# Raw and scaled evictions, token mixing by pairs of tiles, and a new order of steps beside a projection

## The reference

```python
p = p + (token_shift(p) - p) * mu            # token_shift: the row of the token before, 0 for the first
r, k, v, wd, ad, gd = _split(p, (512, 512, 512, 64, 64, 128))
w_log = -softplus(-(w0 + tanh(wd) @ w_up)) - 0.5
decay = exp(-exp(w_log))
a = sigmoid(a0 + ad @ a_up)
g = sigmoid(gd) @ g_up
kk = hd(k * k_k)
kk = kk * rsqrt(maximum(sum(kk * kk, axis=-1), 1e-24))    # keys of unit length, by head of 64
k_mod = hd(k * (1.0 + (a - 1.0) * k_a))
y = rwkv7_scan(r, decay, k_mod, v, -kk, kk * a)           # a recurrence over the tokens
bonus = sum(r * k_mod * r_k, axis=-1) * v
```

## Time and profile before

| | us |
|---|---|
| median of 3 runs | 3233.77 (3233.0 to 3235.81) |
| the profiled execution, its own time | 3229.9 |
| its span in the trace | 3228.1 |
| mean granted clock of TensorE | 0.915 of full |
| TensorE busy | 2859.5 (89% of the span) |
| DVE busy | 1922.0 (60%) |
| ACT busy | 1361.9 (42%) |

### The profile page before, as it was taken

How to read it: one execution, slowest core, us unless ns; L and a number is a source line. 1 busy time by engine, 2 the same in 40 slices (tenths; PEclk the granted TensorE clock), 3 DMA queues, 4 the chain that set the end, 5 groups by cost and what they waited for, 6 DMA issues and landing times. The chain is left out here.

```text
span 3228.1 us, 53616 instructions
## 1 busy us (share of the span) xinstructions
PE 2859.5 (89%) x23052; PEld 2452.1 (76%) x23052; DVE 1922.0 (60%) x2576; ACT 1361.9 (42%) x1873; POOL 151.7 (5%) x116
## 2 busy tenths in 40 slices
PE   7898678999897778999998998889999989988899
PEld 6787557888786657888886875678888878756688
DVE  5754766965655766956555444666565644446564
ACT  5413334645413244645453232545454532325443
POOL 0030000000030000000000310000000012000000
PEclk9998888998898888998998998989999988989899
DMA  5211114564111123555542111245645411203453
GB/s 213 92 40 53 66 54 148 197 212 157 66 43 63 66 81 137 202 187 183 198 144 74 40 66 40 93 143 202 220 170 197 141 64 40 72 34 119 138 201 131
DMA packets 54667, 386.18 MB, mean 120 GB/s; under 512 B 6688, under 2 KB 7328, under 8 KB 8352
## 3 DMA queue, kind: packets, MB, share of 16 engines
q1 hardware_dynamic: 54432, 382.76, 34.5%
HBM read 381.69 MB, written 1.05 MB: 119 GB/s over the span
## 5 line engine op out<-in xcount | busy, mean ns | idle before, releaser
L320 PE MATMUL banks<-normed_high,weights_high 128*128 128x256 f16 (+1 forms) x4096 | 1150.7, 281 | 49.6 <-DVE normed_low L414 22.6
L321 PE MATMUL banks<-normed_low,weights_high 128*128 128x256 f16 (+1 forms) x4096 | 1149.7, 281 | 0.0
L322 PE MATMUL banks<-normed_high,weights_low 128*128 128x256 f16 (+1 forms) x4096 | 1148.1, 280 | 0.0
L306 DVE SCALAR_TENSOR_TENSOR weights_low<-weight_ring,weights_high 128x2048 f16<-128x2048 f32 x334 | 761.1, 2279 | 417.2 <-ACT weights_high L300 402.8
L300 ACT ACTIVATE weights_high<-weight_ring 128x2048 f16<-128x2048 f32 x306 | 580.2, 1898 | 299.3 <-PE banks L322 284.0
L320 PE MATMUL banks<-projected,weights_high 128*128 128x256 f16 x1696 | 471.7, 278 | 73.3 <-DVE projected L331 73.3
L320 PEld LDWEIGHTS banks<-normed_high,weights_high 128*128 128x128 f16 (+1 forms) x4096 | 412.8, 101 | 126.3 <-issue 47.3
L321 PE MATMUL banks<-projected,weights_high 128*128 128x256 f16 x1696 | 471.8, 278 | 0.0
L322 PE MATMUL banks<-projected,weights_low 128*128 128x256 f16 x1696 | 471.3, 278 | 0.0
L322 PEld LDWEIGHTS banks<-normed_high,weights_low 128*128 128x128 f16 (+1 forms) x4096 | 411.9, 101 | 59.6
L321 PEld LDWEIGHTS banks<-normed_low,weights_high 128*128 128x128 f16 (+1 forms) x4096 | 411.3, 100 | 59.2 <-issue 1.8
(11 more groups left out here) (390 smaller groups left out, 3251.8 us busy)
## 6 DMA issues: line engine op xcount, KB each, us to landing
weight_ring<-w SPq DMA_DIRECT2D x356, 1024.0 KB, 4.9
small_weights<-small SPq DMA_DIRECT2D x2, 1280.0 KB, 7.9
constants<-const SPq DMA_DIRECT2D x1, 1601.0 KB, 10.1
weight_ring<-w SPq DMA_DIRECT2D x2, 640.0 KB, 3.8
residual<-xt SPq DMA_DIRECT2D x1, 1024.0 KB, 5.0
small_weights<-small SPq DMA_DIRECT2D x2, 512.0 KB, 10.4
out<-residual SPq DMA_DIRECT2D x4, 256.0 KB, 2.8
parameters<-par SPq DMA_DIRECT2D x2, 115.5 KB, 9.6
```

The source lines that it names most:

```text
L306: nc.vector.scalar_tensor_tensor(out=self.part(self.mem.w_low, g), in0=self.part(self.mem.ring, g), scalar=W_SCALE, in1=self.part(self.mem ...
L320: pe.matmul(out, w_high, high, start=start, stop=False, skip_group_check=skip)
L321: pe.matmul(out, w_high, low, start=False, stop=False, skip_group_check=skip)
L322: return pe.matmul(out, w_low, high, start=False, stop=stop, skip_group_check=skip)
```

## The change

1. For tiles 0 to 13 ACT evicts twice: a raw tile (into `raw`, tiles 18 to 31 of the scratch memory) and a tile scaled by `(1 - mu)` times the constant of the halves, one value for each partition (`keep`, made once by DVE in `mu_kept`).
2. The mixing is `projected[t] += mu * raw[t-1]`, one DVE instruction for a tile and 255 tokens, two tiles after each of the low halves 3 to 9. The difference of all 14 tiles (L1205) and the negation of the first token (L1206) are gone.
3. `keys_squared` goes from 11 to 7 on DVE, `keys_sum` from 10 to 6 on TensorE, `keys_guarded` from 14 to 9, `keys_root` from 13 to 7 on ACT (ahead of `low_rank_in`), `keys_inverse` from 15 to 10, `keys_spread` from 14 to 11. `gates_of_a` goes from 9 to 8 and `exps` from 12 to 11 on ACT; `decays_summed` and `decays_centred` from 12 and 13 to 11 and 12; `keys_mixed` and `bonus_products` to 13, `keys_unit` to 14, `bonus_values` to 15, `operands_near` to 16 on DVE; `bonus_sum` from 15 to 13 on TensorE.
4. Two copies of `operands_far` (L1296) go from DVE to ACT, behind the high halves at the end (`operands_copied`).

```diff
@@ project_stage, DVE
         loaded(dve)
+        for step in beside.vector.get("begin", ()):
+            step(link, say, need)
...
@@ project_stage, ACT
             act.wait_ge(sig("tiles_done"), i + 1)
+            if i == 0 and beside.keep is not None:
+                need("mu_kept", 1)
             for n, (g, c0, m, part, tile) in enumerate(grp):
-                ins = nc.scalar.activation(mem.proj[part:part + m, tile, :],
-                                           mem.ps[part:part + m, i % BANKS, n * T:(n + 1) * T],
-                                           ACT.Copy, scale=PART_X)
+                got, scale = mem.ps[part:part + m, i % BANKS, n * T:(n + 1) * T], PART_X
+                if beside.keep is not None and tile < 14:
+                    nc.scalar.activation(beside.raw[:, tile, :], got, ACT.Copy, scale=PART_X)
+                    scale = beside.keep[:, tile:tile + 1]
+                ins = nc.scalar.activation(mem.proj[part:part + m, tile, :], got, ACT.Copy,
+                                           scale=scale)
...
@@ Rwkv
-        self.vector = {9: [self.shift_low_rank], 10: [self.shift], 11: [self.keys_squared],
-                       12: [self.decays_summed], 13: [self.decays_centred],
-                       14: [self.keys_guarded, self.keys_mixed],
-                       15: [self.keys_inverse, self.bonus_products], 16: [self.keys_unit],
-                       "end": [self.bonus_values, self.operands_near, self.operands_far,
-                               self.operands_state]}
-        self.scalar = {7: [self.low_rank_in], 9: [self.gates_of_a], 12: [self.exps],
-                       13: [self.keys_root], "end": []}
-        self.tensor = {8: [self.low_rank_up], 10: [self.keys_sum], 14: [self.keys_spread],
-                       15: [self.bonus_sum], "end": []}
+        self.keep = cut(14)
+        self.raw = cut.buffer[:, 18 * T:32 * T].rearrange("p (a t) -> p a t", a=14)
+        self.vector = {"begin": [self.mu_kept],
+                       3: [self.shift(0)], 4: [self.shift(2)], 5: [self.shift(4)],
+                       6: [self.shift(6)], 7: [self.shift(8), self.keys_squared],
+                       8: [self.shift(10)], 9: [self.keys_guarded, self.shift(12)],
+                       10: [self.keys_inverse], 11: [self.decays_summed],
+                       12: [self.decays_centred], 13: [self.keys_mixed, self.bonus_products],
+                       14: [self.keys_unit], 15: [self.bonus_values], 16: [self.operands_near],
+                       "end": [self.operands_far, self.operands_state]}
+        self.scalar = {7: [self.keys_root, self.low_rank_in], 8: [self.gates_of_a],
+                       11: [self.exps], "end": [self.operands_copied]}
+        self.tensor = {6: [self.keys_sum], 8: [self.low_rank_up], 11: [self.keys_spread],
+                       13: [self.bonus_sum], "end": []}
...
+    def mu_kept(self, link, say, need):
+        mu = self.mem.par[:, C1["mu"]:C1["mu"] + 14]
+        say(self.nc.vector.tensor_scalar(self.keep, mu, -PART_X, PART_X, ALU.mult, ALU.add), "mu_kept")
+
+    def shift(self, first):
+        def step(link, say, need):
+            need("bank_free", first // 2 + 1)
+            for i in (first, first + 1):
+                p = self.mem.proj[:, i, 1:T]
+                say(self.nc.vector.scalar_tensor_tensor(out=p, in0=self.raw[:, i, 0:T - 1],
+                                                        scalar=self.col("mu", i), in1=p,
+                                                        op0=ALU.mult, op1=ALU.add), "shifted")
+        return step
...
+    def operands_copied(self, link, say, need):
+        for i, (n4, f4) in enumerate(self.halves()):
+            need("near_ready", i + 1)
+            link(self.nc.scalar.copy(f4[:, :, 1, :], n4[:, :, 1, :]))
...
     def low_rank_in(self, link, say, need):
-        need("shifted", 2)
+        need("shifted", 14)
...
     def keys_sum(self, pe, need):
-        need("decay_sigmoid", 4)
         need("kk_squares", 1)
...
     def keys_spread(self, pe, need):
+        need("decay_sigmoid", 4)
         need("kk_inverse", 1)
```

More of the change, by code:

```diff
@@ L1171, in __init__ @@
         self.bonus, self.gate, self.out = mem.y[:, 4:8, :], mem.y[:, 8:12, :], mem.y[:, 0:4, :]
-        self.mixed = cut.buffer[:, 0:14 * T].rearrange("p (a t) -> p a t", a=14)
-        self.vector = {9: [self.shift_low_rank], 10: [self.shift], 11: [self.keys_squared],
-                       12: [self.decays_summed], 13: [self.decays_centred],
-                       14: [self.keys_guarded, self.keys_mixed],
-                       15: [self.keys_inverse, self.bonus_products], 16: [self.keys_unit],
-                       "end": [self.bonus_values, self.operands_near, self.operands_far,
-                               self.operands_state]}
-        self.scalar = {7: [self.low_rank_in], 9: [self.gates_of_a], 12: [self.exps],
-                       13: [self.keys_root], "end": []}
-        self.tensor = {8: [self.low_rank_up], 10: [self.keys_sum], 14: [self.keys_spread],
-                       15: [self.bonus_sum], "end": []}
+        self.keep = cut(14)
[12 more added lines that the diff above has]
+                       13: [self.bonus_sum], "end": []}
     def two(self, b):
@@ L1197, in q64 @@
         return flat(ap).rearrange("p (q t) -> p q t", t=HD)
[L1201 to L1207, removed]
-    def shift(self, link, say, need, tiles=tuple(range(12))):
-        for i in tiles:
-            p = self.mem.proj[:, i, :]
-            say(self.nc.vector.scalar_tensor_tensor(out=p, in0=self.mixed[:, i, :],
-                                                    scalar=self.col("mu", i), in1=p,
-                                                    op0=ALU.mult, op1=ALU.add), "shifted")
+    def mu_kept(self, link, say, need):
[10 more added lines that the diff above has]
+        return step
     def keys_squared(self, link, say, need):
@@ L1288, in operands_near, with halves @@
                              q64(self.p_r), q64(z[7]), ALU.mult))
-        link(V.tensor_tensor(flat(self.bt), flat(z[1]), flat(z[5]), ALU.mult))
-        link(V.tensor_tensor(flat(self.kt), flat(self.p_k), flat(z[5]), ALU.mult))
+        say(V.tensor_tensor(flat(self.bt), flat(z[1]), flat(z[5]), ALU.mult), "near_ready")
+        say(V.tensor_tensor(flat(self.kt), flat(self.p_k), flat(z[5]), ALU.mult), "near_ready")
+    def halves(self):
+        return [[v.rearrange("p a (b q t) -> p (a b) q t", b=2, q=2) for v in pair]
+                for pair in ((self.bt, self.btp), (self.kt, self.ktp))]
+    def operands_copied(self, link, say, need):
+        for i, (n4, f4) in enumerate(self.halves()):
+            need("near_ready", i + 1)
+            link(self.nc.scalar.copy(f4[:, :, 1, :], n4[:, :, 1, :]))
     def operands_far(self, link, say, need):
         V = self.nc.vector
-        for near, far in ((self.bt, self.btp), (self.kt, self.ktp)):
-            n4, f4 = (v.rearrange("p a (b q t) -> p (a b) q t", b=2, q=2) for v in (near, far))
-            link(V.tensor_copy(f4[:, :, 1, :], n4[:, :, 1, :]))
+        for n4, f4 in self.halves():
             link(V.tensor_tensor(f4[:, :, 0, :], n4[:, :, 0, :],
@@ L1318, in gates_of_a @@
     def gates_of_a(self, link, say, need):
-        need("shifted", 14)
         need("up_summed", 3)
@@ L2335, in __init__ @@
         self.ea = self.rows[0:HEADS, 3, 0:1]
+        self.keep = None
         self.vector = {4: [self.gate_sizes], 7: [self.gate_sums],
@@ L2814, in first_block @@
     angles = Angles(nc, mem, p_sig)
-    rwkv.vector[3] = [angles.of_positions, angles.sine_angle]
-    rwkv.vector[5] = [angles.cosine_angle]
+    rwkv.vector[3] += [angles.of_positions, angles.sine_angle]
+    rwkv.vector[5] += [angles.cosine_angle]
     rwkv.scalar[4] = [angles.sines]
```

## The result

Before 3233.64 us (3233.0 to 3235.81, 4 runs), after 3213.43 us (3209.92 to 3215.05, 4 runs): ratio 0.9938, 95% interval 0.9926 to 0.995. That is 20 us faster, where 8.1 were forecast, and outside the range. The profiled execution took 3209.92 us, its span 3208.1 (before 3228.1); the mean granted clock went from 0.915 to 0.918.

A forecast was written before the change was run, and what follows sets the result against it. TensorE, busy in 89% of the span, bounds the kernel through its waits and half clock. Per projection -3.1 + 0.7 - 0.8 = -3.2, twice -6.4, clock -1.7: -8.1, from 3233.8 to 3225.7 us, range 3219.5 to 3231.5.

The forecast's parts named there:

- Part 1: Groups 0 to 6 on ACT: four evictions a group take 1.3 us, hidden in ACT's idle time; cost 0.
- Part 2: Mixing on DVE, two instructions a group: covered by DVE's idle time and the low halves' lead; cost 0.
- Part 3: Keys earlier: TensorE's 3.1 us wait at keys_spread goes, 0.7 is added at low_rank_up; 2.4 us earlier a projection.
- +0.7 at `low_rank_up`: Square root and its table load ahead of the sigmoid lengthen TensorE's wait from 1.6 to 2.3 us in each projection.
- Part 4: End of each projection: ACT with two copies is last, 5.55 us behind the last eviction instead of 6.37; -0.8.
- The clock behind `keys_spread`: Second projection alone: the 1.7 us lost to half clock after the 3.1 us wait are won.
- The step that failed: Half clock behind the wait at low_rank_up, 83 to 89 us, left as it is; no gain or loss counted.
- Rival B: At low_rank_up the longer wait prolongs half clock, 1.5 us lost twice; gain only 3.4, 3230.4 us; chance 0.12.
- Rivals C and D: C: added table switch drains ACT, 3228.3 us, chance 0.03; D: double evictions overload ACT in groups 0 to 6, chance 0.04.

The follow-up runs named there:

- b_root: Kernel before with the square root ahead of exps at group 12 on ACT, guard at 12 and reciprocal at 13 on DVE: 3226.09 us, ratio 0.9982.
- before_again: Kernel before, unchanged, run again for a second profile: 3231.52 us, ratio 1.0004.
- b_pad: Kernel before with two single-column copies added on ACT behind the last high halves of each projection: 3230.28 us, ratio 0.9999.
- b_act_copy: Kernel before with only the two copies of operands_far moved from DVE to ACT, behind the last high halves: 3230.02 us, ratio 0.9996.
- after_again: Changed kernel, unchanged, run again for a second profile: 3210.91 us, ratio 0.994 against the kernel before.
- after_r3: Changed kernel, unchanged, run once more: 3213.33 us, ratio 0.9947 against the kernel before.
- a_dve_copy: Changed kernel with the two copies of operands_far back on DVE: 3214.26 us, ratio 0.9947 against the kernel before.
- a_dve_pad: Changed kernel with two single-column copies added on DVE at the head of operands_far: 3213.7 us, ratio 0.9945 against the kernel before.
- a_root_late: Changed kernel with the square root at group 9 on ACT behind the gates, keys_inverse and keys_spread at 12: 3208.22 us, ratio 0.9928 against the kernel before.
- a_both: a_root_late with the two copies of operands_far back on DVE: 3210.03 us, ratio 0.9934 against the kernel before.
- a_both_pad: a_both with two single-column copies added on ACT behind the last high halves: 3212.01 us, ratio 0.9944 against the kernel before.
- b_up_late: Kernel before with low_rank_up behind group 9 instead of group 8 on TensorE: 3222.07 us, ratio 0.9975.
- b_small16: Kernel before with small constant matmuls behind group 6 of both projections (16 meant, 32 in the trace): 3237.8 us, ratio 1.002.

## Why the prediction was wrong

- *Part 1, evictions twice, hidden.* Right: 1.26 until the high half begins behind four (1.3 taken), no wait for a half in groups 1 to 8.
- *Part 2, the mixing, hidden.* Right: no wait of TensorE for it.
- *Part 3, the wait of 3.1 goes.* Right in both projections. b_root bears its worth out: 3.1 went and 1.6 came, twice, so 3.0, and 1.7 of clock in the second projection; 4.8 were measured.
- *Part 3, +0.7 at `low_rank_up`, twice.* Right in the first (2.3), wrong in the second: 0.9, 0.7 less than before. I took the second projection for a copy of the first; it is not on ACT, where the sines of layer one throw out the square root's table. 1.4 us.
- *Part 4, -0.8 for the tail.* -1.1 and -1.0 at the last wait, 1.26 for the two copies where 1.3 was taken.
- *The clock behind `keys_spread`, -1.7.* Gone in the profile, as forecast. That it stood in the second projection alone was chance: over the six profiles that have the wait of 3.1, half clock followed it in 9 of 12 places (1.7 us of clock each), so its worth is about 2.5 on the average for the two projections.
- **The step that failed:** "The granted clock of 0.50 behind the wait of 1.6 [...] I leave as it is: the new wait of 2.3 ends in the same place." It was there to be won or lost, and it is the largest single part: 3.4 us in each projection of the two profiles, 6.8 in all. The runs put in its place: half clock follows the wait at `low_rank_up` by chance, often when the wait is 1.6 or 2.3 long and never when it is 0.9 or less. Counted over all profiles (each projection counts as one case):

| wait at `low_rank_up` | half clock behind it | kernels |
|---|---|---|
| 1.6 us | 9 of 10 | before, before_again, b_root, b_pad, b_act_copy |
| 2.3 us | 3 of 5 | after, after_again, after_r3, a_dve_copy, a_dve_pad |
| 0.9 us | 0 of 5 | the same five, second projection |
| 0.8 us | 0 of 6 | a_root_late, a_both, a_both_pad |
| none | 0 of 2 | b_up_late |

b_small16 (0.8 twice, none behind it) is left out, since it put other work ahead. The length of the standstill is not the whole cause: b_root's 1.6 at L320 brought none, the 3.1 at `keys_spread` brings it in 9 of 12 cases but for half as long (3.4 us instead of 6.8), and b_small16 had it without a standstill. So what TensorE does next to the wait counts too; how the two work together is not shown. The row of 0.9 is the sure gain: 3.4 us in the second projection, where the prediction had +0.7. That 2.3 shows it less often than 1.6 may be chance (3 of 5 beside 9 of 10); the runs don't tell. The 3.4 won in the first projection are the luck of the profiled execution: after_again, the same program, did not have them.

With this the two projections add up. Second: -3.1 (`keys_spread`) - 0.7 (`low_rank_up`) - 1.0 (tail) - 1.7 - 3.4 (clock) = -9.9, measured -10.2. First: -3.1 + 0.7 - 1.1 - 3.4 = -6.9 in an execution without half clock, measured -7.1; in one that has it (after_again) 3.3 of that are not won. From the forecast to the measurement: 8.1, and 6.8 of clock, 1.4 of wait in the second projection, 0.5 of tail and 2.7 in other stages make 19.5 of the 20.0. The median of after lies 3.5 us above its profiled execution for that reason, it seems: 3209.92 and 3210.06 are the own times of the two profiles without it, 3214.81 that of the one with it.

- *Rival B* had the place right and the sign wrong: the wait for the sigmoid was where the clock was decided, but the clock gave there what I feared it would take. *Rivals C and D* are out: the square root starts 1.29 after its load begins and nothing drains, and the Trainium skill's 1.38 us of draining (ScalarE: Activation LUTs, What ACT_TABLE_LOAD costs) is not in these rows. A gain of more than 14 us had no rival at all, because I priced each stretch at half clock by whether the wait that I cut stood in front of it.
- *The 2.7 us in untouched stages* (mostly 3.7 in delta and fox, less 1.2 in the last two) were in no term. They come through the granted clock too: in fox, TensorE's busy time lost 11.3 us to half clock in the profile of before and 5.1 in that of after, in delta 18.8 and 20.4, in mla of layer four 2.9 and 5.9. What of the change sets that off stays open. In a_dve_pad's profile it was gone with four instructions of no work on DVE, in b_act_copy it didn't come; so neither the copies on ACT nor the number of ACT's instructions is the cause by itself. The number of DVE's instructions is not ruled out.

## What to carry to other kernels

Where the granted clock is at half behind a wait, add its loss to the price of that wait: here 1.6 us of standing still ahead of `low_rank_up` cost 5 (1.6 and 3.4 of clock) in 9 of 10 cases, 0.8 cost 0.8, and the same 1.6 ahead of large products cost 1.6. So look first for short waits in a busy stretch with a low clock behind, and shorten or remove them, even by moving one small product a group later; that alone (b_up_late) made the kernel before 8.6 us faster, where the whole change gave 20. Take the clock's part from several profiles, since one shows only one of its outcomes. Before a term is doubled for a second copy of a stage, check the order in the second copy, above all which function table ACT holds when it gets there.

## What the runs showed of the hardware

- TensorE's clock fell to its lower level (0.50 of full, 1.2 instead of 2.4 GHz) behind a standstill of 1.6 us ahead of `low_rank_up` in 9 of 10 cases and behind 0.8 to 0.9 us in none of 11; behind 1.6 us ahead of large products in none of 2 (b_root). The loss was the same each time, 3.4 us at `low_rank_up`, and 1.7 behind `keys_spread` in 9 of 12 cases. In b_small16 it fell with no standstill, 3 us into a row of 32 small f32 products (2 columns each). The Trainium skill (TensorE: Matmul & The Clock Gate, Part 1) says that the monitor runs free of the kernel; the trace agrees in that one program showed both outcomes at one wait (after and after_again, before and before_again).
- An eviction from PSUM with a scale for each partition takes 0.49 us for 128x256 where a constant takes 0.39, and consecutive ones overlap by 0.1.
- Stages that no edit touched took 2 to 6 us more or less by the granted clock between versions (fox of layer three 67.0 or 72.5, the latter also in a_dve_pad, which adds only copies of one column) and between executions of one kernel (mla of layer four 88.0 or 90.9), so a difference under some 5 us between two versions of this kernel is not yet one between their schedules.
